# Three small SBUF tables made larger, so that the tiles behind them start elsewhere

## The reference, cut to what matters

```python
# first_block, DEPTH = 2 layers
x = x + 0.5 * swiglu(rmsnorm(x), w_gate, w_up, w_down)      # D_FF = 2816
proj = rmsnorm(x) @ w_in                                    # 1024 -> 2560
# self attention (12 heads of 64; chunked with a relative bias, or differential with rope)
# and memory attention (4 heads over 256 memory rows)
x = x + concat(o_self, o_memory) @ w_out
x = x + 0.5 * swiglu(rmsnorm(x), ffn2...)
# second_block, one layer
t = moba_attention(h, a_w_in, a_w_out, rel_bias)            # 8 heads of 128
h = layer_norm(ALPHA * h + t)
f = moe_ffn(h, ...)          # 32 experts of 1024 -> 2 * 1024 -> 1024, top 4 of each row
out = layer_norm(ALPHA * h + f)
```

## The kernel before, in words

| tiles | residue before |
|---|---|
| `raw`, `w_hi`, `w_lo`, `w_free`, `x`, `nat_more`, `ident`, `gcol` | 128 |
| `grow`, `qscale` | 192 |
| `bias_parts`, `h_rows`, `flip`, `wr`, `masks` | 32 |
| `flip_r`, `flip_bf`, `chunk_mask` | 0 |
| `masks_bf`, `lg`; `needles`; `rest`, `share`, `row_stats` | 64; 128; 192 |
| `xT_hi`, `xT_lo`, `a_hi`, `a_lo`, `sig`, `gated`, `act`, `pr`, `qkT`, `prob`, `probT`, `y_hi`, `y_lo`, `m_g`, `pick`, `xs_even`, `xs_odd`, `kept_0`, `kept_1`, `late_raw`, `kept_more`, `ln0_gain` | 64 |

## Time and profile before

### The profile page before, as it was taken

The page is one execution under the profiler, slowest core; times in us unless marked ns, Lnnn a source line. Parts: engine busy times, 40 slices in busy tenths (PEclk is TensorE's granted clock), DMA queues, the critical chain, the costliest instruction groups (busy, mean ns, idle before and its releaser), DMA issues.

```text
span 2080.6 us, 28202 instructions
## 1 busy us (share of the span) xinstructions
PE 1986.6 (95%) x12145; PEld 1376.1 (66%) x12145; DVE 898.8 (43%) x1071; ACT 694.2 (33%) x953; POOL 40.6 (2%) x30
## 2 busy tenths in 40 slices
PE   8999999999999998999999999999999999999996
PEld 7999778999999886999888544443334333434432
DVE  6766666676665787666644311111111111111102
ACT  5545575445555556444444111110001000101101
POOL 2500000000000000000000000000000000000000
PEclk9999999999999998999999999999999999999999
DMA  9554707555555442555377899999999999999996
GB/s 312 200 199 151 233 1 249 196 181 190 175 194 198 174 162 73 171 198 187 104 288 292 358 429 428 427 428 427 427 427 428 427 427 427 427 427 428 427 428 290
DMA packets 165416, 604.26 MB, mean 290 GB/s; under 512 B 9276, under 2 KB 102416, under 8 KB 140516
## 3 DMA queue, kind: packets, MB, share of 16 engines
q1 hardware_dynamic: 165316, 602.83, 74.3%
HBM read 601.71 MB, written 1.09 MB: 290 GB/s over the span
## 4 chain that ended last, share of the span: by engine, by line
PE 68%; DMA 24%; DVE 4%; ACT 3%; issue 1%; SPq 0%; DVEq 0%; ACTq 0%
PE ps L1738 15%; PE ps L1740 14%; PE ps L1739 14%; PE ps L2224 11%; DMA sb_w_free<-in_moe_w_gate_up 5%; PE ps L2244 5%; DMA sb_w_free<-in_moe_w_down 5%; DMA sb_nat_more<-in_moe_w_gate_up 3%; DMA sb_late_raw<-in_moe_w_down 3%; DMA sb_raw<-in_moe_w_down 3%; DMA sb_raw<-in_moe_w_gate_up 3%; PE ps L2194 2%; ACT sb_w_hi L659 1%; DVE sb_w_lo L1066 1%; PE ps L2252 1%
## 5 line engine op out<-in xcount | busy, mean ns | idle before, releaser
L1066 DVE TENSOR_TENSOR sb_w_lo<-sb_raw,sb_w_hi 128x2048 fp32r<-128x2048 f32 x179 | 414.7, 2322 | 254.1 <-ACT sb_w_hi L659 253.7
L659 ACT ACTIVATE sb_w_hi<-sb_raw 128x2048 fp32r<-128x2048 f32 x179 | 341.4, 1913 | 174.4 <-PE ps L1740 163.5
L1738 PE MATMUL ps<-sb_xT_hi,sb_w_hi 128*128 128x256 f32 x1408 | 392.7, 279 | 6.6 <-DVE sb_xT_lo L1090 3.9
L1739 PE MATMUL ps<-sb_xT_lo,sb_w_hi 128*128 128x256 f32 x1408 | 391.0, 278 | 0.0
L1740 PE MATMUL ps<-sb_xT_hi,sb_w_lo 128*128 128x256 f32 x1408 | 390.8, 278 | 0.0
L1738 PEld LDWEIGHTS ps<-sb_xT_hi,sb_w_hi 128*128 128x128 f32 x1408 | 265.0, 188 | 9.3 <-issue 4.5
L1739 PEld LDWEIGHTS ps<-sb_xT_lo,sb_w_hi 128*128 128x128 f32 x1408 | 265.8, 189 | 1.5
L1740 PEld LDWEIGHTS ps<-sb_xT_hi,sb_w_lo 128*128 128x128 f32 x1408 | 265.5, 189 | 0.0
L991 ACT ACTIVATE sb_h_rows<-ps 128x512 f32<-128x512 f32 x32 | 19.2, 599 | 423.4 <-PE ps L2224 423.4
L1620 DVE COPY sb_h_rows<-ps 128x512 f32<-128x512 f32 x31 | 21.4, 691 | 317.6 <-PE ps L2224 317.6
L1738 PE MATMUL ps<-sb_w_hi,sb_xT_hi 128*128 128x512 f32 x384 | 152.8, 398 | 0.3 <-DVE sb_xT_lo L1086 0.2
(11 more groups left out here) (304 smaller groups left out, 2440.4 us busy)
## 6 DMA issues: line engine op xcount, KB each, us to landing
sb_raw<-in_moe_w_gate_up SPq DMA_DIRECT2D x49, 2048.0 KB, 34.6
sb_w_free<-in_moe_w_gate_up SPq DMA_DIRECT2D x46, 2048.0 KB, 34.6
sb_w_free<-in_moe_w_down SPq DMA_DIRECT2D x23, 2048.0 KB, 34.3
sb_raw<-in_moe_w_down SPq DMA_DIRECT2D x23, 2048.0 KB, 34.0
sb_raw<-in_ffn_w_gate SPq DMA_DIRECT2D x44, 1024.0 KB, 5.2
sb_raw<-in_ffn_w_up SPq DMA_DIRECT2D x44, 1024.0 KB, 5.2
sb_raw<-in_ffn_w_down SPq DMA_DIRECT2D x44, 1024.0 KB, 4.9
sb_late_raw<-in_moe_w_gate_up SPq DMA_DIRECT2D x17, 2048.0 KB, 33.4
```

The costliest lines, as they stand in the source:

```text
L659: sc.activation(w_hi[:, c % CUT, :], raw[:, c % RAW, :], ACT.Copy).then_inc(hi_made, 1)
L1066: ve.tensor_tensor(w_lo[:, c % CUT, :], raw[:, c % RAW, :], w_hi[:, c % CUT, :].bitcast(F32), ALU.subtract).then_inc(lo_made, 1)
L1738: pe.matmul(o, l_hi, r_hi, start=start, stop=False)
L1739: pe.matmul(o, l_hi, r_lo, start=False, stop=False)
```

## The change

`gcol` gets 96 columns in place of 80, of which 78 are used as before. `qscale` gets 48 in place of 4. `mean_var` gets 32 columns for each row block in place of 2, and the two instructions that write it now name columns 0 and 1. No other instruction differs, and none is added or taken away.

```diff
-        gcol = sb("gcol", [P, 80])
+        gcol = sb("gcol", [P, 96])
         grow = sb("grow", [P, P])
-        qscale = sb("qscale", [P, 4])
+        qscale = sb("qscale", [P, 48])
...
-        mean_var = sb("mean_var", [P, TB, 2])
+        mean_var = sb("mean_var", [P, TB, 32])
...
-                    ve.bn_aggr(mean_var[:, b, :], row_stats[:, b].rearrange("p a b -> p (a b)")).then_inc(first_ln_step, 1)
+                    ve.bn_aggr(mean_var[:, b, 0:2], row_stats[:, b].rearrange("p a b -> p (a b)")).then_inc(first_ln_step, 1)
...
-                ve.bn_aggr(mean_var[:, 0, :], row_stats[:, 0].rearrange("p a b -> p (a b)")).then_inc(ln_step, 1)
+                ve.bn_aggr(mean_var[:, 0, 0:2], row_stats[:, 0].rearrange("p a b -> p (a b)")).then_inc(ln_step, 1)
```

## The result

The changed kernel takes 2111.31 us (median of 4 runs, 2106.80 to 2113.96), the kernel before 2088.46 us (4 runs, 2083.54 to 2089.05). The ratio is 1.0114 [1.0092, 1.0135]: slower by some 23 us. The four times of the changed kernel follow their mean granted clocks, from 2106.80 us at 0.992 to 2113.96 at 0.989, so a few us of that difference can be the clock's; the two profiled executions, at 0.994 and 0.992, lie 24.4 us apart. Forecast were 2086 us and no change, with a range that ended at 2097.

The account below looks back on a forecast made before the run. It took TensorE's matmuls to bound the first stage and DMA the second from 1200 us on. All terms summed to 0.0 us, giving 2086 us, with a range of 2070 to 2097.

Parts of the forecast that it names:

- The narrow form ... I take 0: First stage, 4224 matmuls streaming 256 columns of `xT` with `w_hi` or `w_lo` loaded: stay at 0.113 us each, 0 change.
- The wide form ... I take 0: First stage, 2208 matmuls streaming 512 columns of weights with `xT` or `a` loaded: stay at 0.228 us each, 0 change.
- TensorE's loads: Loads of stationary pieces on TensorE: at residues 0, 32, 64 and 128 durations lie within 2 ns, so 0 change.
- The rule of 16-byte lines: Engines read SBUF in 16-byte lines; tiles already start at multiples of 32, so padding to 256 buys engines nothing.
- The narrow form gets slower: Rival: `xT` streamed from 0 meets `w` loaded from 128; 0.0065 us on 4224 matmuls, 27 us, 2113; chance 0.09.
- The wide form gets faster: Rival: loaded piece at 64 has a hidden cost that residue 0 ends; up to 22 us, down to 2064; chance 0.15.
- The ring: Eight slots receiving DMA chunks; only `late_raw` moves, to residue 0: taken as 0, bound 1.2 us.
- The copies: VectorE and ScalarE copies: ScalarE's into `h_rows` go from 599 to 591 ns, VectorE's stay 691; 0 us of span.
- The count: Whole kernel: the profile after would show the same 28202 instructions.
- the small matmuls: Some 60 matmuls using `flip_r`, `flip_bf`, `chunk_mask`, `masks_bf` at residues 224 or 32: 0.6 us at 10 ns each, taken as 0.
- The stage logic: Second stage lasts as long as its DMA bytes take, plus 21.6 us; a change in the first stage shows in full.
- The base of 2086: Unchanged kernel's time: mean of four times, 2085.7 us, said as 2086.

Follow-up runs that it names:

- xT_lo_to_0: Kernel before with only `xT_lo` moved, from residue 64 to 0: 2103.31 against 2088.12 us, ratio 1.0082.
- a_to_0: Kernel before with `xT` left at residue 64 and `a` and the tiles behind it moved to 0: 2088.39 against 2086.42 us, ratio 1.0007.
- middle_to_0: Changed kernel with `mean_var` enlarged again: middle tiles (`h_rows`, `bias_parts`, `masks`) at residue 0, late tiles back at 64; 2087.87 us, 1.0002 to the kernel before.
- late_to_0: Kernel before with only the late tiles (`xT`, `a` and their like) moved, from residue 64 to 0: 2106.60 against 2085.05 us, ratio 1.0095.
- w192_late64: Kernel before with a pad ahead of `raw` and one ahead of the late tiles: `w` at residue 192, `xT` and `a` at 64; 2111.85 us, ratio 1.0117.
- a_to_128: Kernel before with `xT` left at residue 64 and `a` and the tiles behind it moved to 128: 2097.10 against 2086.42 us, ratio 1.0051.
- late_to_192: Kernel before with the late tiles (`xT`, `a` and their like) moved from residue 64 to 192, `w` at 128: 2104.94 us, ratio 1.0088.
- late_to_128: Kernel before with the late tiles (`xT`, `a` and their like) moved from residue 64 to 128, `w` at 128: 2105.04 us, ratio 1.0094.

## Why the prediction was wrong

**"The narrow form ... I take 0" is the step that failed.** It held that the load of the stationary piece sets the pace and the `xT` stream has slack. The evidence was that 128 moving columns took 0.11 us and 256 took 0.113. That shows that halving the stream gains nothing; it doesn't show that a badly placed stream costs nothing. The bursts of 128 columns hide it: with `flip_r` at another distance after the change they step at 111 ns as before, while those of 256 go from 119.1 to 117.5. With `xT` at 0 under `w` at 128 the narrow form lost 4.5 ns on each of 4224 matmuls, 19 us; only `xT_lo` at 0 was enough for 118.7 ns (xT_lo_to_0), and only `a` at 0 left it at 114.1 (a_to_0).

**"The wide form ... I take 0" failed too**, by 3.1 ns on 2208, 6.8 us. The price that it names, 10 ns, was three times too large and of the wrong sign for this change: the 4% over the expert stage's 0.218 is not undone by residue 0. The one residue that improves the form is 128, by 1.9 ns.

**Both rest on one faulty test.** "TensorE's loads" compared durations at four residues and found them within 2 ns. They still are after the change, at a pace 4% slower; over all runs the narrow form's loads average 188 to 192 ns. The cost lies between one matmul's start and the next, and belongs to a pair of operands; a table of single operands can't hold it. The rule of 16-byte lines, taken from the Trainium skill ("SBUF — State Buffer", "Door 1: The DMA port swizzle"), agrees with the loads' and copies' durations here and says nothing of pairs; the paces show an effect among starts that are all multiples of 32.

**The rival "The narrow form gets slower" named the right pair and the right sign**, with a chance of 0.09. That the two reads meet is its explanation, and no run shows that. It read the cost off the one place where 0 met 128, `flip_r`, and priced it at 6.5 ns and 2113 us; measured were 4.5 ns there, 3.1 ns in the wide form, and 2111.3. That the two times are so near is luck: the price was too high for the narrow form and left the wide one out. It was read off one of the trace's four bursts of 256 columns; without the first step of each, the eight steps of all four average 119.1 ns, which is 4.7 above the narrow form's 114.4 and would have given 20 us, where the narrow form lost 19. What was held against it, that bursts of four have other matmuls around them, was a reason for a wider range and not for dismissal: the row was the only one at the new distance, and it pointed one way. It decided from 1.5 ns on, and three times that came.

**The rival "The wide form gets faster"** fell. Its guess that the load's duration hides a cost was true, and the sign wrong.

**The ring: right.** 428 GB/s and 33.4 and 34.0 us to landing, as the earlier trace rows. The estimate after the Trainium skill ("DMA: Bandwidth & Descriptors", "How a descriptor splits into AXI transactions"), 0.5 us over the 24 chunks of `late_raw` when their rows start at a multiple of 256, doesn't show; it is too small for these runs to refute.

**The copies: right but for one.** VectorE's copy into `h_rows` stayed at 691. ScalarE's stayed at 599 ns too, where 591 was foretold, so the 8 ns to `m_g` don't come from the residue of either. **The count, the loads and the small matmuls** are as foretold; middle_to_0 bounds the middle tiles at 0.15%.

**The stage logic: right.** The first stage's loss of 25.3 us came through to the end as 24.3, because the second stage lasts as long as its bytes. The base of 2086 was right as well: the medians of the kernel before were 2085.05 to 2088.46.

## What to carry to other kernels

Before operands are moved in SBUF, count the starts of the dominant matmul form, take the pace from start to start and not from durations, and look for any place in the trace where a pair already meets at the new distance. Padding that looks free can cost 1% when TensorE never waits, and the busy share won't show it: compare matmuls per 100 us. Try the handful of 32-byte steps on the chip, look at every dominant form in each, since moving one form's operand can slow the other, and keep what measures best; neither "aligned to 256" nor "far apart" was a good guide here.

## What the runs showed of the hardware that was not expected

**The pace of back-to-back float32r matmuls depends on the distance between the starts of what is streamed and what is loaded**, modulo 256, and on more than that. Over the eight places it varies by up to 5% in the narrow form (114.4 to 120.0 ns) and 3% in the wide (227.4 to 234.1), with loads of 188 to 192 ns. Placements with the same distance and other residues agreed within 0.6 ns, when `xT` and `a` moved together. That TensorE's two reads hinder each other is a reading of this and was not shown, nor why one distance should be better than another.

**At the same addresses the narrow form has two steady rhythms.** In the kernel before, 38 of 45 unbroken groups of 29 to 143 matmuls run at about 113.6 ns and 7 at 117.8, each for the group's whole length. Timeline of the kernel before, a group of the slow kind and the next one:

```profile
357.94 0.28 PE L1738 MATMUL ps<-sb_xT_hi,sb_w_hi 128*128 128x256 f32 x1
...
359.00 0.28 PE L1738 MATMUL ps<-sb_xT_hi,sb_w_hi 128*128 128x256 f32 x1
...
374.95 0.28 PE L1738 MATMUL ps<-sb_xT_hi,sb_w_hi 128*128 128x256 f32 x1
...
375.97 0.28 PE L1738 MATMUL ps<-sb_xT_hi,sb_w_hi 128*128 128x256 f32 x1
```

1.06 / 9 = 0.118 and 1.02 / 9 = 0.113. At distance 128 there are two as well, 118.6 and 120.0, the same in the changed kernel, late_to_0 and w192_late64. In middle_to_0 17 of 45 groups are slow, a whole feed-forward among them. In a_to_128 it is 42 of 44, and there neither of the narrow form's operands has been moved, only `a`, the loaded piece of the wide form that runs between the groups, and the tiles behind it. So something outside the pair can pick the rhythm. What ran just before isn't enough to tell it: in middle_to_0 the fourth feed-forward is slow throughout and the third is fast from its third group on, with the same instructions between the groups.

This could also be why the kernel before varies from run to run (2079 to 2099 us over all its runs) more than late_to_192, whose groups all run at 117.8 (2104.3 to 2105.5): a feed-forward with its 1056 narrow matmuls in the slow rhythm costs 1056 x 4.2 ns = 4.4 us. That is only argued, since no run without a profile shows its paces, and there is a rival: the granted clock. late_to_128, whose groups all run at 119.9 in its trace, still varies from 2103.6 us (clock 0.992) to 2108.5 (0.990), and the 2099 us of the kernel before had the lowest clock of all its runs, 0.987.

The rhythms also mean that about three quarters of the narrow form's loss at distance 128 could be described as the fast rhythm no longer being found, and the rest, from 117.8 to 119, as a slower one; the runs don't separate the two. How the rhythm is chosen stays open.
